# Short convolution's input projection: B's column pairs 1 to 3 as seven block products, weights streamed C, B, U, and the norm's factor applied behind W_out

## The reference

```python
def short_conv_mixer(h, w_in, conv_w, w_out):
    bcx = h @ w_in
    b_gate = bcx[..., :D_MODEL]
    c_gate = bcx[..., D_MODEL:2 * D_MODEL]
    xp = bcx[..., 2 * D_MODEL:]
    u = c_gate * xp
    u_conv = lax.conv_general_dilated(
        u, conv_w[:, None, :].astype(u.dtype), window_strides=(1,),
        padding=[(CONV_WIDTH - 1, 0)], dimension_numbers=('NWC', 'WIO', 'NWC'),
        feature_group_count=D_MODEL)
    return (b_gate * u_conv) @ w_out
```

## Time and profile before

| | |
|---|---|
| median of three runs | 1054.05 us (1053.57 to 1055.11) |
| profiled execution, its own time | 1053.88 us |
| its span in the profile | 1051.7 us |
| TensorE busy | 1044.6 us, 99% |
| VectorE busy | 894.4 us, 85% |
| ScalarE busy | 544.2 us, 52% |
| weights and other data read | 103.59 MB |
| convolution's input on TensorE | about 536 to 663 us |
| W_out on TensorE | about 663 to 706 us |

### The profile page before, as it was taken

The page is one execution under the profiler, slowest core; times in us unless marked ns, Lnnn a source line. Parts: engine busy times, 40 slices in busy tenths (PEclk is TensorE's granted clock), DMA queues, the critical chain, the costliest instruction groups (busy, mean ns, idle before and its releaser), DMA issues.

```text
span 1051.7 us, 18190 instructions
## 1 busy us (share of the span) xinstructions
PE 1044.6 (99%) x6910; PEld 957.6 (91%) x6910; DVE 894.4 (85%) x1270; ACT 544.2 (52%) x778; POOL 46.5 (4%) x28
## 2 busy tenths in 40 slices
PE   9999999999999999999999999999999999999998
PEld 8888888899999999889888888888999999988897
DVE  6787775999999998996979668689999999899685
ACT  6678884745554555633343323365455545563432
POOL 0342230000000000000000000000000000000000
PEclk9999999999999999999999999999999999999999
DMA  8121212233233222223223232232332232223212
GB/s 340 52 71 50 75 45 80 81 121 115 87 117 120 93 106 110 80 103 118 93 98 120 80 120 81 93 108 81 120 120 88 111 120 99 91 99 122 81 70 80
DMA packets 16970, 106.26 MB, mean 101 GB/s; under 512 B 1888, under 2 KB 2272, under 8 KB 6432
## 3 DMA queue, kind: packets, MB, share of 16 engines
q1 hardware_dynamic: 16416, 104.60, 27.7%
q10 hardware_dynamic: 432, 0.83, 0.2%
q0 software_dynamic: 80, 0.26, 0.1%
HBM read 103.59 MB, written 2.10 MB: 100 GB/s over the span
## 4 chain that ended last, share of the span: by engine, by line
PE 91%; DVE 6%; ACT 1%; issue 1%; DVEq 0%; ACTq 0%
PE bank L510 29%; PE bank L512 29%; PE bank L511 29%; PE bank L683 1%; DVE x_lo L1829 1%; DVE split L1488 1%; DVE acc L1519 1%; PE bank L571 1%; DVE s_lo L1869 0%; PE bank L668 0%; PE bank L671 0%; ACT split L1217 0%; DVE split L1866 0%; DVE rstd L1524 0%; DVE head L1775 0%
## 5 line engine op out<-in xcount | busy, mean ns | idle before, releaser
L510 PE MATMUL bank<-x_hi,split 128*128 128x256 f32 (+1 forms) x704 | 203.6, 289 | 0.0
L512 PE MATMUL bank<-x_hi,split 128*128 128x256 f32 (+1 forms) x704 | 203.6, 289 | 0.0
L511 PE MATMUL bank<-x_lo,split 128*128 128x256 f32 (+1 forms) x704 | 203.6, 289 | 0.0
L511 PEld LDWEIGHTS bank<-x_lo,split 128*128 128x128 f32 x704 | 132.4, 188 | 2.6
L510 PEld LDWEIGHTS bank<-x_hi,split 128*128 128x128 f32 x704 | 132.4, 188 | 2.6
L512 PEld LDWEIGHTS bank<-x_hi,split 128*128 128x128 f32 x704 | 132.4, 188 | 2.5
L510 PE MATMUL bank<-x_hi,s_hi 128*128 128x256 f32 x480 | 134.5, 280 | 0.1
L512 PE MATMUL bank<-x_hi,s_lo 128*128 128x256 f32 x480 | 134.0, 279 | 0.0
L511 PE MATMUL bank<-x_lo,s_hi 128*128 128x256 f32 x480 | 134.0, 279 | 0.0
L1866 DVE TENSOR_TENSOR split<-raw,split 128x2048 fp32r<-128x2048 f32 x51 | 116.8, 2289 | 15.2 <-ACT split L1217 13.7
L1217 ACT ACTIVATE split<-raw 128x2048 fp32r<-128x2048 f32 x51 | 97.7, 1916 | 60.9 <-DVE work L1861 49.4
(11 more groups left out here) (285 smaller groups left out, 2375.9 us busy)
## 6 DMA issues: line engine op xcount, KB each, us to landing
raw<-weights_in SPq DMA_DIRECT2D x82, 1024.0 KB, 4.8
raw<-weights_in SPq DMA_DIRECT2D x12, 768.0 KB, 4.2
work<-x SPq DMA_DIRECT2D x4, 512.0 KB, 12.7
raw<-weights_in SPq DMA_DIRECT2D x4, 512.0 KB, 3.7
out<-head SPq DMA_DIRECT2D x3, 512.0 KB, 2.7
head<-head_in SPq DMA_DIRECT2D x1, 768.0 KB, 9.2
first_raw<-weights_in SPq DMA_DIRECT2D x3, 192.0 KB, 5.3
first_raw<-weights_in SPq DMA_DIRECT2D x1, 576.0 KB, 7.9
```

What stands on the lines that cost most here:

```text
L510: pe.matmul(o, lhs[0], rhs[0], start=start, stop=False, skip_group_check=True)
L511: pe.matmul(o, lhs[0], rhs[1], start=False, stop=False, skip_group_check=True)
L512: return pe.matmul(o, lhs[1], rhs[0], start=False, stop=stop, skip_group_check=True)
```

## The change

The B chunks of pairs 1, 2 and 3 become seven block products in banks 0 to 3; pair 0's B stays plain. The stream order per pair becomes C, B, U, and on TensorE C, B, U as well. For a B block product the banks are not all opened (waited for as drained) at the start: the third and the fourth are opened at their first product. B is stored without `rstd`; that factor is applied to W_out's result in `mixer_out`, two multiplications of 128x512 ahead of the two additions. The high part `u_hi` of the convolution's result is made by ScalarE (`mixed_hi`) instead of VectorE, right behind the taps; VectorE makes the rest (`mixed_rests`).

The diff's core, with everything that the sections below speak of:

```diff
@@ block(tensor)
-            def winograd(s, b0, x_of=x_block, sums_of=None):
+            def winograd(s, b0, x_of=x_block, sums_of=None, in_turn=False):
...
-                for b in range(b0, b0 + 4):
+                for b in (p, q) if in_turn else (p, q, r, t):
                     open_bank(b)
...
                 block_product(q, block_sums, 0, X_T1, True).then_inc(product_done[5], 1)
+                if in_turn:
+                    open_bank(r)
                 block_product(r, blocks, 2, X_B21, True).then_inc(product_done[2], 1)
...
+                if in_turn:
+                    open_bank(t)
                 block_product(t, blocks, 3, X_T4, True)
...
-            for c in range(0, 12, 3):
-                chunk(c % 2, [0, 1], A, ready=None if c else made)
-                if c == 0:
+            for pair in range(K_PAIRS):
+                s = pair % 2
+                chunk(s, [2, 3], A, ready=None if pair else made)
+                if pair:
+                    winograd(1 - s, UP_BANK, conv_block, in_turn=True)
+                else:
                     stat(6, KD)
-                chunk((c + 1) % 2, [2, 3], A)
-                if c == 0:
+                    chunk(1, [0, 1], A)
                     pe.wait_ge(x_split, T.add("x", K_PAIRS))
-                winograd(c % 2, GATE_BANK, conv_block)
+                winograd(s, GATE_BANK, conv_block)
@@ block(scalar)
+            for pair in range(1, K_PAIRS):
+                s = pair % 2
+                blocks_hi(1 - s)
+                sums_hi_of(1 - s)
+                taps(2 * pair - 2)
+                mixed_hi(2 * pair - 2)
...
+                copy(1, 1)
+                copy(1, 5)
                 blocks_hi(s)
                 sums_hi_of(s)
+                copy(1, 6)
+                copy_last(1, 1 - s)
                 split(1 - s)
                 copy(0, 1)
                 copy(0, 5)
                 copy(0, 6)
                 copy_last(0, s)
@@ block(vector)
-            def mixer_out(all_banks):
+            def mixer_out(all_banks, scale=None):
...
                     for h, b in enumerate(banks):
-                        add_result(b, 2 * c + h)
+                        if scale is not None:
+                            do(v.tensor_tensor(tile(work, h), bank[b][:, :], scale, ALU.mult))
+                    settle()
+                    for h, b in enumerate(banks):
+                        add_result(b, 2 * c + h, None if scale is None else tile(work, h))
...
+            drained_part(mix_y, 2, rstd2)
+            done(1)
+            for b in range(2):
+                drain(b, v.tensor_copy(mix_b[b], bank[b][:, :]))
+            landed(0, 1)
+            split(1)
+            next_forms(0)
+            top_left(0, u_half)
+            top_right(0, u_half)
+            for pair in range(1, K_PAIRS):
+                s = pair % 2
+                corners(1 - s)
+                forms_split(1 - s)
+                conv_mix(2 * pair - 2)
+                done(s)
                 drained_part(mix_y, 2, rstd2)
+                mixed_rests(2 * pair - 2)
+                next_forms(s)
+                top_left(1, b_half)
+                forms_split(s)
+                top_right(1, b_half)
+                corners_b(1 - s)
                 split(1 - s)
+                if pair < K_PAIRS - 1:
+                    next_forms(s)
                 top_left(0, u_half)
                 top_right(0, u_half)
@@ weight_stream
-                for part in range(3):
+                for part in (1, 0, 2):
                     chunk = columns(w["conv_w_in"][0], span(part * D + m * 2 * P))
-                    yield block_order(chunk) if part == 2 else chunk
+                    yield block_order(chunk) if part == 2 or part == 0 and m else chunk
```

More of the change, by code:

```diff
@@ L354, in build @@
         part_summed, u_made = sem("part_summed"), sem("u_made")
+        mix_made = sem("mix_made")
         gate_scaled, result_added = sem("gate_scaled"), sem("result_added")
@@ L1398, in taps, with mixed_hi @@
                     act.activation(mix_y[b], mix_u[b], ACT.Copy, scale=tap(CONV - 1, m + b)).then_inc(taps_started, 1)
[L1400 to L1404, removed]
+            def mixed_hi(m):
+                for b in range(2):
+                    act.wait_ge(mix_made, m + b + 1)
+                    take(tile(u_hi, m + b), mix_b[b])
+            blocks_hi(0)
+            sums_hi_of(0)
+            split(1)
+            copy(0, 1)
+            copy(0, 5)
+            copy(0, 6)
+            copy_last(0, 0)
+            banks_used(dict(b0=1, b1=1, b2=1, b3=1, b5=1, b7=1))
+            for pair in range(1, K_PAIRS):
[4 more added lines that the diff above has]
+                mixed_hi(2 * pair - 2)
+                banks_used(dict(b2=1, b3=1))
+                copy(1, 1)
+                copy(1, 5)
                 blocks_hi(s)
                 sums_hi_of(s)
+                copy(1, 6)
+                copy_last(1, 1 - s)
                 split(1 - s)
@@ L1411, in _ @@
                 copy_last(0, s)
+                banks_used(dict(b1=1, b3=1, b5=1, b7=1))
             split(1)
             taps(KD - 2)
-            banks_used({f"b{b}": 4 for b in (0, 1, 2, 3, GATE_BANK + 1, GATE_BANK + 3)})
+            mixed_hi(KD - 2)
             mixer_out(CONV_OUT_BANKS, "ffn_norm1")
@@ L1771, in _, with add_result @@
             heads((HEADS - 2) * SEQ)
-            def add_result(b, m):
-                drain(b, v.tensor_tensor(at(xT, m), bank[b][:, :], at(xT, m), ALU.add))
+            def add_result(b, m, scaled_result=None):
+                drain(b, v.tensor_tensor(at(xT, m), bank[b][:, :] if scaled_result is None else scaled_result, at(xT, m), ALU.add))
             def add_scaled(b, m):
@@ L1949, in winograd_round, with mixed_rests @@
                 inner_product(f, 1, (UP_BANK + 3,))
-            def inner_operands(f, tiles):
+            def mixed_rests(m):
                 for b in range(2):
[L1953 to L1956, removed]
+                    taken()
+                    ready(lo(tile(u_lo, m + b), mix_b[b], tile(u_hi, m + b)))
+                all_ready()
             def inner_rests(ms):
@@ L2163, in conv_mix @@
                 for b in range(2):
[L2164 to L2167, removed]
+                    v.tensor_tensor(mix_b[b], mix_b[b], mix_y[b], ALU.mult).then_inc(mix_made, 1)
+                v.wait_ge(mix_made, m + 2)
             def drained_part(tiles, b0, scale):
@@ L2173, in drained_part, with b_half, corners_b, next_forms @@
                 landed(b0, b0 + 1)
+            def b_half(m, half):
+                return mix_b[m][:, half * HT:(half + 1) * HT]
+            def corners_b(s):
+                done(s)
+                b = UP_BANK
+                v.wait_ge(drained[b], T.add(f"b{b}"))
+                do(v.tensor_tensor(b_half(1, 1), copies[1][0], copies[1][1], ALU.add))
+                drain(b + 3, v.tensor_tensor(b_half(1, 0), bank[b + 3][:, 0:HT], copies[1][0], ALU.add))
+                settle()
+                landed(b + 1, b + 2, b + 3)
+            def next_forms(s):
+                for n in range(2):
+                    wait(v, sums_split[n], T.now(f"sums{n}"))
+                forms(s)
             forms(0)
@@ L2183, in _ @@
             settle()
[L2184 to L2195, removed]
-                drained_part(mix_y, 2, rstd2)
+            drained_part(mix_y, 2, rstd2)
+            done(1)
+            for b in range(2):
+                drain(b, v.tensor_copy(mix_b[b], bank[b][:, :]))
+            landed(0, 1)
+            split(1)
+            next_forms(0)
[6 more added lines that the diff above has]
+                conv_mix(2 * pair - 2)
+                done(s)
+                drained_part(mix_y, 2, rstd2)
+                mixed_rests(2 * pair - 2)
[4 more added lines that the diff above has]
+                corners_b(1 - s)
                 split(1 - s)
+                if pair < K_PAIRS - 1:
+                    next_forms(s)
                 top_left(0, u_half)
@@ L2202, in _ @@
             conv_mix(KD - 2)
+            mixed_rests(KD - 2)
             clear_acc()
-            mixer_out(CONV_OUT_BANKS)
+            mixer_out(CONV_OUT_BANKS, rstd[:, :])
             ffn(None)
```

## The result

| | before | after |
|---|---|---|
| median | 1053.84 us (1053.46 to 1055.11, six executions) | 1058.47 us (1058.34 to 1059.92, six) |
| ratio | | 1.0045, 95% interval 1.0032 to 1.0058 |
| profiled execution, its own time | 1053.88 us | 1059.92 us |
| its span | 1051.7 us | 1058.0 us |
| mean granted clock | 0.999 | 0.998 |

The change costs 4.63 us where 2.56 was forecast. It is slower, as forecast, but 0.3 us above the upper end of the range.

What follows compares the result with a forecast made beforehand. TensorE, busy 99% at full clock, was taken to set the time: -3.30 + 2.68 + 2 x 0.92 + 0.90 + 0.44 = +2.56 us on 1054.05 gives 1056.6 us (+0.24%), range 1054.4 to 1058.2.

Steps and rivals of the forecast that it cites:

- The saving: Three B chunks on TensorE go from 48 matmuls of 512 columns to 84 of 256: 1.10 us each, 3.30 in all.
- Pair 1's wait: TensorE waits 2.68 us before B's last product in pair 1, for ScalarE's late copy of product 6.
- The copies out of PSUM: Pair 1's plain copies of B: 0.69 us each, like the drains; at 0.42 each the chain is 0.5 us shorter.
- the third bank: Pair 1: drained at about 581.6, wanted at 581.77, so no wait; any loss there shortens the next wait equally.
- Pairs 2 and 3: In B's block product a chain of 9.32 us against 8.40 to hide it: TensorE waits 0.92 us per pair.
- W_out: Last pair: two multiplications add 1.34 us on VectorE, so TensorE waits 0.90 us for the split of the sum of squares.
- Starting again: After each of four waits TensorE's first matmul holds the second back 0.11 us, 0.44 in all.
- TensorE's clock falls behind pair 1's wait: Rival, chance 0.02: half clock over U's block product behind the wait, 9.80 us more, 1066.4 us.
- From 565.28 on VectorE never stops: Pair 1: VectorE's unbroken work, then ScalarE's splits and copy, take 24.77 us, to 590.05.
- The rival with waits half as long: TensorE's waits about half as long, +1.07 us, 1055.1 us, called no change; chance 0.37.

Runs made afterwards that it cites:

- e2: Changed kernel with U's forms ahead of `u_lo` (`mixed_rests`) in VectorE's order; median 1053.61 us, ratio 0.9994.
- e3: Changed kernel with ScalarE's copy of B's product 6 ahead of the split of U's blocks; median 1056.67 us, ratio 1.0027.
- e8: e2 with ScalarE's copy of B's product 6 between the split of U's blocks and that of U's sums; median 1054.44 us, ratio 0.9991.
- e4: Changed kernel without the two multiplications by `rstd` in each pair of W_out, the factor left out altogether; median 1057.42 us, ratio 1.0031.
- e7: Kernel before with only the norm's factor of B moved behind W_out; median 1055.77 us, ratio 1.0015.
- e9: The changed kernel run once more, nothing altered; median 1059.32 us, ratio 1.0049.
- e5: e8 with, in W_out's last pair, the channel mixer's next weight split first on ScalarE and right behind VectorE's additions; median 1053.03 us, ratio 0.9983.
- e10: e5 with 20 small chained ScalarE operations holding back pair 2's copy of product 6; median 1058.99 us, ratio 1.0043.

## Why the prediction was partly right

- **The saving: right.** -1.10 us for each of three chunks. Pair 2 closes with it to 0.02 us. With the 1.19 a chunk that the Trainium skill's rule gives ("TensorE: Matmul & The Clock Gate", "Back-to-back issue gap") it would be off by 0.11; the trace's 0.117 and 0.227 hold.
- **Pair 1's wait: right in size, in part by luck.** 2.68 forecast, 2.65 measured. The copies out of PSUM cost 1.29 for two, the upper bound that I had taken. But two misses of 0.22 us cancel in it (the third bank, below).
- **Pairs 2 and 3: right.** 0.92 forecast, 0.96 measured, by e2, e3 and e8 for the reason given: U's forms behind C's drain, and ScalarE's queue behind the forms.
- **W_out: right as far as it went.** 0.90 forecast and measured; e4 and e7 show that the multiplications make it.
- **Starting again: right.** 0.10 to 0.11 for each of the four waits.
- **"TensorE's clock falls behind pair 1's wait": the step that failed.** I gave it 0.02 and left it out of sum and range. It came in all four profiles whose wait was 2.64 us or longer, and by the clocks in nine of twelve executions of this kernel. Its size was off too: I priced a whole block product at half clock, 9.80 us, and it was 17 matmuls, 1.55 us. What I had cited from the Trainium skill ("TensorE: Matmul & The Clock Gate", "What's actually happening"), that idleness brings back the lower clock, agrees with these traces, and "2.7 us is longer than anything the trace shows" was a reason to take it into the range, not to leave it out.
- **"From 565.28 on VectorE never stops": wrong by 0.22 us.** The third bank costs TensorE 0.22, and as the prediction said, this makes the next wait shorter by as much, since pair 1's wait ends by VectorE's and ScalarE's chain, which doesn't stop for it (C's drain starts at 582.72, 2.2 us behind the C chunk's end). But the chain is longer too: 566.83 to 591.82 is 24.99 us instead of 24.77. VectorE waits 0.19 at 572.63 for ScalarE's copy of U's last product, and from the first quarter to U times C (571.69 to 573.42) it takes 1.73 us where 0.68 + 0.79 was laid out. The same 0.19 stands in e9 and e5. No run takes it away, so the term rests on the traces.
- **Not in the sum: the channel mixer's first rounds.** W_out's lateness leaves VectorE behind, and a copy that was 0.07 late before is 0.39 late: 0.32 us, gone in e4 and in e5.

1.55 + 0.22 + 0.32 = 2.09 is what was missed: 2.56 + 2.09 = 4.65, and the medians differ by 4.63. That they agree so well is in part chance, since the changed kernel's median lies among executions with the fall and executions with a slow loop in its place; the traces' 4.70 is the firmer number. The rival with waits half as long fell; each wait had nearly its full length. (Its sum had taken away only W_out's wait and 0.5 us of pair 1's.) The range reached down to 1054.4 for it, and the room was needed above.

What stays open: why a loop of the channel mixer runs 1% slower in some executions of every kernel here, before included, why e7's times are 0.7 us higher than expected, and what decides whether an execution of after goes without the fall of the clock.

## What to carry to other kernels

Where a change adds a wait to a TensorE that was never idle for so long, price two things: the wait, and the clock behind it. Then lay out what the wait stands behind: here moving one group of instructions on VectorE, one copy on ScalarE and one split on both turned +4.6 us into -2.1. The wait was in an engine's order and not in its amount of work. Compare single terms between cuts at the same matmuls in two traces; medians carry drifts of 1.6 us that have nothing to do with the change.

## What the runs showed of the hardware

- In four profiles a wait of 2.64, 2.65 (twice) or 2.96 us on TensorE was followed by matmuls at 1.2 GHz (0.213 us apart instead of 0.117), for 17, 17, 17 and 12 matmuls, at a cost of 1.1 to 1.55 us. Where the fall begins varies at the same length of wait: 0.2 us behind the restart in e4, 0.6 in after, 1.0 in e9; in e10 it came while TensorE still waited. Waits of 1.31 and 1.92 us were not followed by it in their profiles.
- It doesn't come each time: by the mean granted clock, in nine of twelve executions with the wait of 2.65 us, in four of five with 2.96, and in one of eleven with 1.92. Filled with 20 matmuls that nobody reads, the same wait left the clock full in both profiles and at 0.999 or more in all eleven executions.
- The same loop with the same granted clock can run 1% slower for some 170 us, in one execution and not in the next.
- A chain of one-element copies on ScalarE, each waiting for the one before, took 4.64 us for 20: 0.23 us each.
